# Modulation of layer 0 in 24 blocks of 512 columns, with the scan branch projected in two halves of the contraction

## The reference, cut to what matters

```
m = silu(cond) @ mod_w[i] + mod_b[i]            # two conditioning rows; mod_w is 2 x (1024 x 6144)
h = rms_norm(x, g) * (1 + scale) + shift        # shift, scale: the first two of the six vectors
xb = h @ w_in                                   # 1024 x 2560: columns 0..1279 gate, 1280..2559 scan branch
gate = gelu(xb[..., :1280]);  xr = centred_conv(xb[..., 1280:], conv_w, conv_b)
r, i = sigmoid(block_diag(xr, ...)) x2 directions          # 16 blocks of 80 x 80
y = scan forwards + scan backwards
out = ((y_f + y_b) * gate) @ w_out              # 1280 x 1024
x = x + gate_vector * rms_norm(out, g)
then: router, top-8 of 64 experts, shared expert, routed experts (3 MB of float32 weights each)
```

## Time and profile before

| | us |
|---|---|
| median of 3 runs | 1532.89 |
| lowest and highest | 1524.75, 1533.18 |
| the profiled execution: its time | 1533.19 |
| its span, first to last instruction | 1531.4 |
| PE busy in the span | 1356.6 (89%) |
| DVE, ACT busy | 484.3, 359.3 |
| read from HBM | 503.13 MB, 330 GB/s over the span |
| mean granted clock of PE | 0.953 |

### The profile page before, as it was taken

One profiled execution on the slowest core, in us unless ns is written; L12 is line 12 of the kernel. 1 busy time (PEld: TensorE's weight loads), 2 busy tenths in 40 slices (PEclk: granted clock), 3 DMA queues, 4 the chain that ended last, 5 costly groups with the idle time before them and its releaser, 6 DMA issues.

```text
span 1531.4 us, 24288 instructions
## 1 busy us (share of the span) xinstructions
PE 1356.6 (89%) x9674; PEld 695.7 (45%) x9727; DVE 484.3 (32%) x1233; ACT 359.3 (23%) x719; POOL 12.2 (1%) x11
## 2 busy tenths in 40 slices
PE   5899987599999898899997987799999898899995
PEld 2777743364444343344433455364444343344432
DVE  2655600323332222223223226243322222223223
ACT  2157120221212121111223025222212121111223
POOL 2000000000000000000000000000000000000000
PEclk8999997799999999999999997899999999999998
DMA  9864767958999999999995322758999999999991
GB/s 361 258 222 184 280 236 280 372 203 327 421 421 420 420 419 421 421 420 421 420 367 193 110 83 83 271 222 332 420 420 420 419 420 421 420 421 421 420 389 58
DMA packets 104434, 506.84 MB, mean 331 GB/s; under 512 B 18633, under 2 KB 23302, under 8 KB 54406
## 3 DMA queue, kind: packets, MB, share of 16 engines
q1 hardware_dynamic: 102592, 501.32, 81.4%
q0 software_dynamic: 608, 2.11, 0.3%
q10 hardware_dynamic: 1126, 1.84, 0.3%
HBM read 503.13 MB, written 2.11 MB: 330 GB/s over the span
## 4 chain that ended last, share of the span: by engine, by line
PE 67%; DMA 22%; ACT 5%; DVE 3%; issue 2%; SPq 2%; ACTq 0%; DVEq 0%
PE PS L668 65%; DMA ring<-in_moe_w_up 18%; DMA ring<-in_mod_w 2%; DMA diag<-in_shared_w_gate 2%; SPq L497 2%; PE PS L676 1%; ACT W L1376 1%; ACT W L1321 1%; PE PS L879 0%; DVE sst L2064 0%; DVE diag L1566 0%; ACT ring L1283 0%; PE PS L1133 0%; SPq L491 0%; DVE diag L2082 0%
## 5 line engine op out<-in xcount | busy, mean ns | idle before, releaser
L668 PE MATMUL PS<-ring,W 128*32 128x512 f32 (+3 forms) x2936 | 617.2, 598 | 5.1 <-DMA ring<-in_moe_w_up 3.1
L668 PE MATMUL PS<-W 128*128 128x128 bf16 (+5 forms) x3316 | 509.8, 369 | 28.6 <-DMA ring<-in_moe_w_up 14.8
L668 PEld LDWEIGHTS PS<-W 128*128 128x128 bf16 (+3 forms) x3318 | 228.8, 107 | 210.7 <-issue 163.5
L668 PEld LDWEIGHTS PS<-ring,W 128*32 128x32 f32 (+2 forms) x2936 | 175.8, 123 | 195.5 <-issue 184.4
L668 PE MATMUL PS<-W,junk 128*128 128x128 bf16 x848 | 117.0, 220 | 24.8 <-ACT W L1376 24.8
L1804 DVE COPY W<-PS 128x512 f32<-128x512 f32 x53 | 36.7, 692 | 277.4 <-PE PS L668 277.4
L1810 DVE TENSOR_TENSOR hT<-PS,hT 128x512 f32<-128x512 f32 x106 | 73.3, 692 | 154.5 <-ACT hT L1385 154.4
L668 PE MATMUL PS<-ring,hT 128*128 128x512 f32 x256 | 112.2, 601 | 2.4 <-DVE hT L1541 1.6
L668 PE MATMUL PS<-hT,W 128*128 128x512 bf16 x373 | 100.2, 385 | 13.9 <-issue 8.0
L1385 ACT CAST hT<-PS 128x512 bf16<-128x512 f32 x106 | 62.1, 586 | 197.8 <-PE PS L668 197.8
L1787 DVE SCALAR_TENSOR_TENSOR W<-W,PS 128x256 f32<-128x256 f32 x53 | 25.5, 480 | 237.2 <-ACT W L1372 237.2
(11 more groups left out here) (250 smaller groups left out, 888.6 us busy)
## 6 DMA issues: line engine op xcount, KB each, us to landing
ring<-in_moe_w_gate SPq DMA_DIRECT2D x106, 1024.0 KB, 19.4
ring<-in_moe_w_up SPq DMA_DIRECT2D x106, 1024.0 KB, 23.0
ring<-in_moe_w_down SPq DMA_DIRECT2D x106, 1024.0 KB, 21.5
ring<-in_mod_w SPq DMA_DIRECT2D x32, 1152.0 KB, 10.3
W<-in_moe_w_gate SPq DMA_DIRECT2D x24, 1024.0 KB, 14.7
W<-in_moe_w_up SPq DMA_DIRECT2D x24, 1024.0 KB, 17.7
W<-in_moe_w_down SPq DMA_DIRECT2D x24, 1024.0 KB, 19.9
ring<-in_mod_w SPq DMA_DIRECT2D x16, 768.0 KB, 13.3
```

The costliest lines, as they stand in the source:

```text
L668: return eng.matmul(out, lhsT, rhs, start=first, stop=last, skip_group_check=True)
```

## The change

All 2 x 6144 columns of the modulation now go in 24 blocks of 512 columns (2 MB each), twelve per layer, each with 8 matmuls of 512 columns and 4 small ones. The order of the first four is 0, 2, 1, 3: blocks 0 and 2 hold the first half of shift and of scale, that is what the first four k-rows of `hT` need. From block 4 on the sums alternate between banks 4 and 5, and block m waits for the copy of m-2. The rows of sums have four places in ring slot 0 (from 3 on) instead of places of other tiles; copies of late blocks are all ACT's.

The scan branch is projected in two phases: phase A takes k-rows 0 to 3 for all ten chunks (five banks, two chunks to a bank), phase B k-rows 4 to 7 and closes the sums. The load of `w_in`'s right half is cut likewise (`winA`, `winB`). ACT takes two chunks at a time out of PSUM; DVE convolves them. The gelu branch (`gelu_in`) uses five banks.

Of the row vectors only `c_ctx`, `c` and `norm_g` are loaded by ACT and turned first; the seven others, the router's bias and `attn_lambda` are loaded by POOL and turned after two blocks.

```diff
-MB = 768
+MB = 512
+MODS = 24
-EARLY = 3
+EARLY = 4
-PROLOGUE = [("mod0", 0), ("mod1", 1), ("mod2", 2), ("win0", 3), ("win1", 0), ("win2", 2), ("mod3", 3), ("win3", 0),
-            ("mod4", 3), ("mod5", 3), ("mod6", 1), ("mod7", 3), ("wout0", 2), ("mod8", 1), ("mod9", 3), ("wout1", 0)]
-PROLOGUE += [(f"mod{m}", 3 if m % 2 else 1) for m in range(10, 16)]
+PROLOGUE = [("mod0", 0), ("mod2", 1), ("winA", 2), ("mod1", 3), ("mod3", 0), ("winB", 1), ("mod4", 0), ("gel0", 2),
+            ("gel1", 1), ("mod5", 0), ("mod6", 3), ("mod7", 0), ("mod8", 3), ("wout0", 2), ("mod9", 0), ("mod10", 3),
+            ("wout1", 1), ("mod11", 0)]
+PROLOGUE += [(f"mod{m}", 0 if m % 2 else 3) for m in range(12, MODS)]
-FIRST_BANKS = (4, 5, 7, 3)
+FIRST_BANKS = (5, 5, 7, 7)
...
-            for m in range(EARLY):
-                load_mod(m)
-            load_win(0)
+            load_mod(0)
+            load_mod(2)
+            load_win("A")
+            load_mod(1)
+            eng.wait_ge(s.mod_summed, 1)
+            load_mod(3)
+            eng.wait_ge(s.mod_summed, 2)
+            load_win("B")
             load_gates(0)
-            eng.wait_ge(s.mod_summed, 1)
-            load_win(1)
             load_gates(1)
...
+            eng.wait_ge(s.mod_summed, 4)
+            load_mod(4)
+            eng.wait_ge(s.win_done, 1)
+            load_gel(0)
+            eng.wait_ge(s.win_done, 1 + KR // 2)
+            load_gel(1)
+            eng.wait_ge(s.mod_summed, 5)
+            load_mod(5)
             eng.wait_ge(s.gate_summed, 4 * KR)
             load_mod(6)
...
-            for m in range(10, 16):
+            for m in range(11, MODS):
                 eng.wait_ge(s.mod_summed, m - 1)
                 load_mod(m)
-            moe_loads(0, [("router", (s.wout_half, 1)), (4, (s.state_ready, 1)), (1, (s.mod_summed, 15)),
-                          (3, (s.mod_summed, 16)), (0, (s.mixer_done, 2)), ("shared", (s.xT_turned, 8)),
+            moe_loads(0, [("router", (s.wout_half, 1)), (4, (s.state_ready, 1)), (3, (s.mod_summed, MODS - 1)),
+                          (1, (s.mixer_done, 2)), ("shared", (s.xT_turned, 8)), (0, (s.mixer_done, 2)),
                           (2, (s.logits_done, 1))])
...
             wout(0, 0, KR)
-            for m in (10, 11, 12, 13):
-                sum_mod(m)
-                if m > 10:
-                    turn_mod(m - 1)
+            more_mods(12, 20)
             wout(1, 0, 3)
-            turn_mod(13)
-            sum_mod(14)
-            turn_mod(14)
-            sum_mod(15)
+            more_mods(20, 22)
             wout(1, 3, 5)
-            turn_mod(15)
+            more_mods(22, MODS)
+            turn_mod(MODS - 1)
```

More of the change, by code:

```diff
@@ L1354, in _ @@
             rms_of_y(0, 0)
[L1355 to L1356 removed]
+            for m in range(12, 16):
+                copy_mod(m)
             rms_of_x(1, 0)
[L1358 to L1359 removed]
+            for m in range(16, MODS):
+                copy_mod(m)
             eng.wait_ge(s.state_turned, 1)
@@ L1595, in _, with copy_rows @@
-            eng.wait_ge(s.vecs_ready, 1)
+            def copy_rows(first, end):
+                for i, (n, at) in list(enumerate(ROW_TILES))[first:end]:
+                    ins = eng.tensor_copy(vecs[:, i, 0:n], PS[:, 7, at:at + n])
+                ins.then_inc(s.vecs_ready, 1)
+            eng.memset(condT[:, :, :], 0.0).then_inc(s.vecs_ready, 1)
+            eng.wait_ge(s.vecs_turned, 1)
+            copy_rows(0, 1)
+            eng.wait_ge(s.consts_loaded, 16)
+            dve.keep(eng.tensor_copy(ident16, ident))
@@ new lines, in _, with copy_mod, adaln_vectors @@
+            dve.keep(eng.tensor_scalar(minus16, ident, -1.0, None, ALU.mult))
+            def copy_mod(m):
+                eng.wait_ge(s.mod_summed, mod_at(m) + 1)
+                mod_place_free(eng, m)
+                eng.tensor_copy(mod_rows(m), PS[:, mod_bank(m), :]).then_inc(s.mod_dve, 1)
+            def adaln_vectors(first, end):
+                lo, hi = 4 * first, 4 * end
+                dve.keep(eng.tensor_tensor(modT.rearrange("p i m s -> p (i m) s")[:, lo:hi],
+                                           PS[:, 6 + first // 12, turned(lo):turned(lo) + 2 * (hi - lo)]
+                                           .rearrange("p (m s) -> p m s", s=NS),
+                                           bc(vecs[:, 1, lo:hi], 2, NS), ALU.add))
+                dve.settle()
@@ new lines, in input_gain, with first_input @@
+            def input_gain(n, k=0, end=KD):
+                L, q = divmod(n, 2)
+                dve.keep(eng.scalar_tensor_tensor(out=amod[:, n, k:end],
+                                                  in0=modT[:, L, 24 * q + 8 + k:24 * q + 8 + end],
+                                                  scalar=1.0, in1=bc(gvec(L, 2 * q)[:, k:end], 2, NS),
+                                                  op0=ALU.add, op1=ALU.mult))
+            def first_input(half):
+                eng.wait_ge(s.mod_done, 2 * (half + 1))
+                adaln_vectors(half, half + 1)
+                adaln_vectors(2 + half, 3 + half)
+                input_gain(0, 4 * half, 4 * half + 4)
+                dve.settle()
+                eng.tensor_copy(lam[:, 7:8], epsc).then_inc(s.early_ready, 1)
+                input_of(0, half)
@@ L1641, in input_gain @@
-            def input_gain(n):
-                L, q = divmod(n, 2)
-                dve.keep(eng.scalar_tensor_tensor(out=amod[:, n], in0=modT[:, L, 24 * q + 8:24 * q + 16],
-                                                  scalar=1.0, in1=bc(gvec(L, 2 * q), 2, NS),
-                                                  op0=ALU.add, op1=ALU.mult))
-            copy_mod(0, 1)
-            for st in range(NS):
-                normed(0, st)
-            for m in (1, 2):
-                copy_mod(m, 1)
```

346 lines of the change are left out of this document (177 added, 169 removed).

## The result

The changed kernel takes 1548.78 us (median of 4 runs, 1545.84 to 1550.39) against 1528.82 (4 runs, 1523.98 to 1533.18) of the kernel before on the same chip: ratio 1.0129, 95% interval 1.0086 to 1.0173. It is slower by 1.3%. Its profiled execution has a span of 1547.4 us against 1531.4, a difference of 16.0 where the medians give 20.

A forecast was written before the change was run, and what follows sets the result against it. Transfers pace the experts' loop, and mostly PE's own work ahead sets its first refill. Front -4.5, middle +4, behind stream 0 +22, seam -11.3 gave +10: span 1531.4 to about 1541.6, forecast 1543 us, range 1526 to 1558.

The forecast's parts named there:

- the front: Start to block 5's sum: -4 at the last forward gate, -0.5 for smaller turnings among the backward gates.
- the seam: Mixer's end to first gathering: -11.3, the 9.56 wait for the shared expert's weights goes and later groups speed up.
- Rival 3: Block transfers: small pieces move slower, 345 GB/s, adding 8 to 13, so 1551 to 1556; chance 0.25 together with rival 4.
- Behind stream 0: Stream 0's projection end to stream 1's: +22, ten blocks must come one by one through two slots.
- the ledger: Block-by-block times behind stream 0's projection, ending at 83.8: +23.7, or +18.2 with PE warm throughout.
- five chunks of w_out and the norm turns 10.1: Last step behind stream 0's projection, from the last turnings at 73.7 to 83.8.
- rival 1: Behind stream 0's projection: transfers keep ahead and PE's work of 54 bounds it, -6 instead of +22, total 1515; chance 0.07.
- Block 0 lands at 12.9: Start of the front: first modulation block lands 1.05 MB earlier, at 12.9 instead of 15.52.
- The wait for ACT's decays stays: Behind the forward gates: PE's wait for ACT at 114.43 was to remain.
- The middle: Block 5's sum to the gate vector's broadcast: +4, seven blocks instead of five in two slots.
- rival 4: Seam: shared weights stay late, so it gives only 3, total 1551; chance 0.25 together with Rival 3.
- gain about 1.8: Seam: the two slow-clock groups behind the wait for the shared weights get about 1.8 faster.

The follow-up runs named there:

- e7: Changed kernel with modulation blocks 12 to 23 going round three slots instead of two: 1531.8 us, ratio to the kernel before 1.0003.
- e6: Changed kernel with each modulation block fetched as two 1 MiB transfers instead of three smaller ones: 1543.7 us, ratio to the kernel before 1.0083.
- e2: Changed kernel with expert 0 put back ahead of the shared expert's weights: 1551.9 us, ratio to the kernel before 1.0161.
- e5: Changed kernel with modulation blocks 14 to 23 neither loaded nor waited for: tail 52.2 us against 85.9; median 1489.5, not comparable.
- e8: Changed kernel with two of the convolution's three multiply-add taps on DVE left out: 1519.4 us, not comparable (fewer experts read).
- e4: Changed kernel with the nine small loads issued by ACT behind x instead of by POOL: 1545.6 us, ratio to the kernel before 1.0122.
- e12: Changed kernel with block 11's load ahead of the second w_out load on SP's queue: 1538.8 us, ratio to the kernel before 1.0050.
- e3: Changed kernel with the sums of blocks 12 and 13 inside stream 0's output projection instead of behind it: 1544.8 us, ratio to the kernel before 1.0110.
- e1: Kernel before with the shared expert's weights issued ahead of expert 0: 1523.6 us, ratio to the kernel before 0.9970.
- e9: Kernel before with the shared expert's weights ahead of expert 0 and blocks 12 to 15 round three slots: 1510.7 us, ratio to the kernel before 0.9876.
- e10: As e9, with block 10 also summed inside stream 0's output projection: 1512.2 us, ratio to the kernel before 0.9882.
- e11: Changed kernel with three slots, two-piece blocks, small loads by ACT, and blocks 12 and 13 summed early, copies ahead: 1525.8 us, ratio to the kernel before 0.9980.

## Why the prediction came out as it did

**Direction and range.** Slower, at 1548.8, inside 1526 to 1558, 5.8 above the 1543. That is 1.3% where I gave "within 1%" 0.60 and "slower" 0.32: the less likely case. The 5.8 flatter the forecast: it was +10 on a median of 1532.9, and with a fourth run that median became 1528.8, so the difference of the medians is 20.0, twice what I said. The two profiled executions differ by 16.0, of which 14.9 have come by the gathering. Three terms were mis-sized: the front and the tail cost 3.0 and 3.9 more than forecast, the seam gave 2.8 more, so they cancel in part. Rival 3 does not explain the miss: the bytes flowed at 386 to 388 GB/s, not 345 (e7, e6).

**Behind stream 0 (+22, measured +25.9): right in mechanism, and the ledger was better than the value taken.** The ledger, the prediction's list of blocks, had block 14's sum end 14.7 behind the projection, block 17's 32.8, block 19's 45.6, block 23's 71.2, the last turnings 73.7. Measured: 13.7, 32.3, 45.0, 70.2, 73.7. What failed is the step "five chunks of w_out and the norm turns 10.1": it priced them at the full clock, and three of them took 7.88 for 5.3 at 297.12, in a window at 0.50. The step took 12.2; the ledger's +23.7 and these 2.1 make the +25.9 but for rounding. That is no accident of one profile: the three chunks take 7.7 to 8.2 in four of the five kernels with this tail and 5.31 only in e2, whose tail is the shortest (80.8). Over the means the tail's term is +26.3. The choice of +22, nearer to a warm PE, had no row for it. e5 shows the cause (52.2 without transfers; rival 1's "54" was the right size of PE's work, for a case that needs the transfers gone), e7 the kind: slots that come free too late for the bytes to flow under stream 0's projection, and then their round trip.

**The front (-4.5, measured -1.5 in this pair, -3.1 over the means).** The steps held in kind: phase A closed by a wait of 1.93, the gates waiting for DVE (2.3; e8: 2.9). Three sizes failed. "Block 0 lands at 12.9" was 16.30, since POOL's loads do not cost nothing (e4: 13.08); but the second block, for which I had 19.7, comes at 21.64 and in e4 still at 20.64, so most of that loss is not POOL's. The convolution took what I said (23.6 for ten chunks) but began at 66.14 instead of 63.3. And "The wait for ACT's decays stays": it grew from 3.29 to 5.39. ACT's work moved up by 2.2, as the last forward gate did, while PE reached the wait 4.3 earlier, since a turning less and a smaller sum stand ahead of it: the -0.5 for them went into the wait. PE gained 5.1 at the first gate (85.1 to 80.0), 2.2 at the last forward gate and 2.2 at the first gate behind the decays.

**The middle (+4, measured +4.4, +6 over the means)**, with its reason: "block 11 lands at +63" was 62.7. What I took as the price of seven blocks in two slots was for the greater part one place in SP's queue (e12).

**The seam (-11.3, measured -14.1).** The shared weights were no longer waited for, so rival 4 falls, and the 9.56 came in full. The term was too small in "gain about 1.8": the two groups behind the wait ran at the low clock before, and at the full one they give 3.1. The groups ahead of it gave another 1.4, most of it in the sixteen turning matmuls behind the router's, 2.93 and now 1.97. Timelines of PE, before and then changed:

```profile
294.41 2.93 PE L946 MATMUL PS<-con,hT 128*128 128x128 f32 x16
...
310.87 3.19 PE L668 MATMUL PS<-junk,minus 128*128 128x512 bf16 x4
```

```profile
323.11 1.97 PE L989 MATMUL PS<-con,hT 128*128 128x128 f32 x16
...
327.08 1.88 PE L686 MATMUL PS<-junk,minus 128*128 128x512 bf16 x4
```

The routing moved up too, from 24.2 to 22.9 behind the mixer's end, and PE shows no wait for it.

**What the change does as a whole.** The tail holds 6144 columns instead of 4608, two more sums and turnings of the old size, 8.4 us of PE (2.79 and 1.40 each). They come out of the stretch ahead of the broadcast, which nevertheless is not shorter (mean over the kernels with the changed front and middle, changed, e2, e3, e5, e7: 197.0; old front, before, e1, e9, e10: 194.2), since the convolution, the decays and block 11 hold it. So the work that was moved bought nothing where it left and cost transfers where it went: ten blocks of 2.1 MB must come behind the projection instead of four of 3.15, 8.4 MB more, 21 us at 400 GB/s. Whether 24 blocks without this move, with the old number of columns behind stream 0, would cost anything wasn't tried, nor e12's middle and e11's tail in one kernel.

## What to carry to other kernels

When blocks of weights go round a few slots, write the ledger per block (release, issue, bytes, landing, use at the clock that a waiting PE gets) and believe it; what PE does right behind such a stretch is also paid at the low clock. Before making the pieces smaller, look for one more slot and for a load that stands in the queue ahead of what is needed first: here these two were worth 17 and 10 us of the medians, a few lines each. And give a stage that is read from one profile its spread first: the same tail took 80.8 to 88.7 us in five kernels. A gain at the head of the program counts only as far as the engines behind it, here DVE's convolution and ACT's decays, move up too.
